# Gating unit's second half and all heads' values by seven block products, with a new order of retention

## What is computed

```python
h = _rmsnorm(x, g_pre_mix)
q, k, v, g, u, sv, gate_r, gate_s = split(h @ w_in)
# retention, 4 heads: q, k 128 wide, v, g 256 wide
o = _layernorm(retention(rotary(q), rotary(k), v))      # both directions, decay by distance
ret = (o * silu(g)) @ w_ret_o
# gating unit: u and sv are 1024 wide
u = gelu(u)
sv = _layernorm(gelu(sv), sgu_ln_g, sgu_ln_b)
sgu = (u * (w_spatial @ sv + b_spatial)) @ w_sgu_o      # mixes tokens within 128
x = x + rmsnorm(mixture of ret and sgu by sigmoid gates @ w_out)
x = x + rmsnorm(conv-gated mlp)
```

## Time and profile before

| what | value |
|---|---|
| median of the timed runs | 2129.3 us |
| time of the profiled execution | 2129.32 us |
| its span, first to last instruction | 2127.5 us |
| TensorE matmuls busy | 2117.5 us, 12356 |
| VectorE busy | 1698.5 us |
| ScalarE busy | 1098.1 us |
| share of TensorE in the chain that ended last | 96% |
| mean granted clock of TensorE | 0.999 |

### The profile page before, as it was taken

The page is one execution under the profiler, slowest core; times in us unless marked ns, Lnnn a source line. Parts: engine busy times, 40 slices in busy tenths (PEclk is TensorE's granted clock), DMA queues, the critical chain, the costliest instruction groups (busy, mean ns, idle before and its releaser), DMA issues.

```text
span 2127.5 us, 32016 instructions
## 1 busy us (share of the span) xinstructions
PE 2117.5 (100%) x12356; PEld 1854.2 (87%) x12356; DVE 1698.5 (80%) x2623; ACT 1098.1 (52%) x1824; POOL 135.4 (6%) x181
## 2 busy tenths in 40 slices
PE   9999999999999999999999999999999999999998
PEld 7888889999888888889999888888888899888887
DVE  7999988888867999988888866664766569877887
ACT  5788555555535788555555534332554344222354
POOL 0010001111010010001111010000000000000000
PEclk9999999999999999999999999999999999999999
DMA  5221246775333221237775333223232231222552
GB/s 196 71 82 63 91 122 177 179 194 152 110 114 112 74 79 63 97 117 178 180 189 155 110 114 129 99 79 118 91 107 70 99 139 46 99 93 98 188 178 99
DMA packets 61331, 252.64 MB, mean 119 GB/s; under 512 B 7520, under 2 KB 8288, under 8 KB 42784
## 3 DMA queue, kind: packets, MB, share of 16 engines
q1 hardware_dynamic: 47680, 223.72, 29.8%
q0 software_dynamic: 13248, 27.27, 7.8%
q10 hardware_dynamic: 288, 0.14, 0.0%
HBM read 245.19 MB, written 2.10 MB: 116 GB/s over the span
## 4 chain that ended last, share of the span: by engine, by line
PE 96%; DVE 2%; ACT 1%; DMA 0%; issue 0%; SPq 0%; DVEq 0%; ACTq 0%
PE mm L2780 20%; PE mm L2782 20%; PE mm L2781 20%; PE sp L2780 9%; PE sp L2782 9%; PE sp L2781 9%; PE ob L3065 1%; PE sp L3037 1%; PE sp L3052 1%; DVE conv_y L1757 1%; PE ob L3045 0%; PE sp L3054 0%; ACT probs L820 0%; PE misc L2780 0%; PE misc L2782 0%
## 5 line engine op out<-in xcount | busy, mean ns | idle before, releaser
L2780 PE MATMUL mm<-in_hi,w_hi 128*128 128x512 f32 (+1 forms) x1536 | 541.6, 353 | 0.4 <-DVE in_lo L1679 0.4
L2781 PE MATMUL mm<-in_lo,w_hi 128*128 128x512 f32 (+1 forms) x1536 | 536.7, 349 | 0.0
L2782 PE MATMUL mm<-in_hi,w_lo 128*128 128x512 f32 (+1 forms) x1536 | 536.7, 349 | 0.0
L2780 PEld LDWEIGHTS mm<-in_hi,w_hi 128*128 128x128 f32 x1536 | 288.9, 188 | 41.2 <-issue 3.4
L2782 PEld LDWEIGHTS mm<-in_hi,w_lo 128*128 128x128 f32 x1536 | 288.7, 188 | 37.8
L2781 PEld LDWEIGHTS mm<-in_lo,w_hi 128*128 128x128 f32 x1536 | 289.0, 188 | 36.1
L764 ACT ACTIVATE w_hi<-w_raw 128x2048 fp32r<-128x2048 f32 (+2 forms) x103 | 192.2, 1866 | 226.3 <-PE mm L2782 187.0
L1645 DVE TENSOR_TENSOR w_lo<-w_raw,w_hi 128x2048 fp32r<-128x2048 f32 (+1 forms) x102 | 224.6, 2201 | 87.2 <-ACT w_hi L764 78.9
L1013 ACT ACTIVATE w_hi<-w_raw 128x512 fp32r<-128x512 f32 x206 | 126.7, 626 | 188.7 <-DVE w_raw L2059 88.2
L2780 PE MATMUL sp<-in_hi,w_hi 128*128 128x256 f32 (+1 forms) x544 | 177.7, 327 | 0.0
L2782 PE MATMUL sp<-in_hi,w_lo 128*128 128x256 f32 (+1 forms) x544 | 177.4, 326 | 0.0
(11 more groups left out here) (574 smaller groups left out, 4849.0 us busy)
## 6 DMA issues: line engine op xcount, KB each, us to landing
w_raw<-in_w_dram SPq DMA_DIRECT2D x134, 1024.0 KB, 4.8
w_raw<-in_w_dram SPq DMA_DIRECT2D x85, 512.0 KB, 6.1
w_raw<-in_w_dram POOLq DMA_DIRECT2D x44, 256.0 KB, 4.2
w_third_sum<-in_w_dram SPq DMA_DIRECT2D x44, 256.0 KB, 6.4
w_third_sum<-in_w_dram POOLq DMA_DIRECT2D x44, 256.0 KB, 4.8
w_raw<-in_w_dram SPq DMA_DIRECT2D x8, 768.0 KB, 4.2
w_chain<-in_w_dram SPq DMA_DIRECT2D x6, 1024.0 KB, 6.5
w_chain<-in_w_dram POOLq DMA_DIRECT2D x4, 1024.0 KB, 9.4
```

Source lines behind the costliest of these rows:

```text
L2780: MM(out, ah, bh, start=first, stop=False, **kw)
L2781: MM(out, ah, bl, start=False, stop=False, **kw)
L2782: return MM(out, al, bh, start=False, stop=last, **kw)
```

## The change

- **sv and v** are each made by seven block products (Strassen's form) instead of eight: TOK_A11, A12, S1, S2, S4, S3, A22. A block has 256 tokens (two halves i of 128), four k-tiles and 512 columns. Some operands on the token side are x itself; four others (`token_operand_at`, o = 0 to 3) are sums and differences of x's quarters, made in `tks`, `tkh` and `tkl`: for each pair of k-tiles p one difference, one scaled copy, three sums, a high part each and a low part each. On the weight side S1 and S3 are sums made by accumulating loads (`tok_chain`), S2 and S4 are sums made by VectorE (`tok_first_sum`, `tok_second_sum`). The products are put together by ScalarE copies (`tok_copy`) and VectorE additions (`tok_take`), or by accumulating in the bank.
- **Order**: u's tiles 0 to 3 come first, with the square sum in the second one; then sv, then the values of all four heads (`token_matrix(1, TOK_V)`), then u's tiles 4 to 7. The last down product of the second layer gets the first instructions for the new operands in between.
- **The variance** of sv is taken between two weight parts of the values; the four normalisations are spread behind it. The centring of the values and the decay tables move beside the gating unit's output.
- **Retention** loses its value products. q and k of the next head stand ahead of the weighing of this head; score weights are made for two token blocks at once in a tensor of their own (`rpf`), and the outputs are copied out of the banks by ScalarE, not VectorE.
- **SP and POOL**: loads of the two matrices wait for semaphores of their own; POOL issues four accumulating loads of 1 MB. There are as many weight chunks as before.

The diff, cut to its core:

```diff
-S_SV, S_U, S_SGU, S_RET, S_AR, S_RO, S_OUT, S_UP, S_DOWN = 4, 4, 8, 12, 4, 4, 4, 22, 14
+S_SV, S_V, S_U, S_SGU, S_RET, S_AR, S_RO, S_OUT, S_UP, S_DOWN = 4, 4, 4, 8, 8, 4, 4, 4, 22, 14
...
+TOK_SV, TOK_V, TOK_END = 2, 9, 16
+TOK_A11, TOK_A12, TOK_S1, TOK_S2, TOK_S4, TOK_S3, TOK_A22 = range(7)
+DOWN_DONE = 7 * FT + D_SPOTS
+PLAIN_DONE = 7 * FT + D_SPOTS - N_SPOTS
...
+            e.wait_ge(s_sm, (DEPTH - 1) * DOWN_DONE + PLAIN_DONE)
+            sv_w, v_w, u_w = n + 2, n + 2 + S_SV, n + 2 + S_SV + S_V
...
+            for i in range(2):
+                tok_load(tok_chain[i], sv_w + 2, s_k[i])
...
-            for t, src in ((gtab, SGT[:, 0:D]), (btab, SGT[:, D:2 * D]), (bsp, sg[:, 0]), (wspr, sg[:, 1])):
+            for t, src in ((btab, SGT[:, D:2 * D]), (bsp, sg[:, 0]), (wspr, sg[:, 1])):
...
+            e.wait_ge(s_w, made(0))
+            tok_load(raw[:, 0, :], sv_w, s_raw[0])
+            e.wait_ge(s_w, made(1))
+            tok_load(raw[:, 1, :], sv_w + 1, s_raw[1])
+            e.wait_ge(s_mmf, DEPTH * L_MM + 2 + 1)
+            e.dma_start(gtab, SGT[:, 0:D]).then_inc(s_tab, 16)
+            e.wait_ge(s_bs, 1)
+            tok_load(raw[:, 0, :], sv_w + 3, s_raw[0])
+            e.wait_ge(s_w, made(TOK_SV + TOK_S1))
+            tok_load(tok_chain[0], v_w + 2, s_k[0])
+            e.wait_ge(s_bs, 2)
+            tok_load(raw[:, 1, :], v_w, s_raw[1])
+            e.wait_ge(s_w, made(TOK_SV + TOK_S3))
+            tok_load(tok_chain[1], v_w + 2, s_k[1])
+            e.wait_ge(s_w, made(TOK_SV + TOK_A22))
+            tok_load(raw[:, 0, :], v_w + 1, s_raw[0])
...
+            sv_w = DEPTH * L_CHUNKS + 2
+            for m, c in enumerate((sv_w, sv_w + S_SV)):
+                for i, part in ((0, 3), (1, 0)):
+                    e.wait_ge(s_k[i], 16 * (m + 1))
+                    e.dma_start(tok_chain[i], W[c + part:c + part + 1].rearrange("a p c -> (a p) c"),
+                                accum_op=ALU.add).then_inc(s_ka[i], 16)
...
+                def token_first_high(p):
+
+                    e.wait_ge(s_td, p + 1)
+                    e.activation(tkh[:, p, 0, :], tks[:, p, 1, :], ACT.Copy,
+                                 scale=minus_gn[:, 2 * p:2 * p + 1]).then_inc(s_t1, 1)
+                    e.activation(tks[:, p, 2, :], x[:, 2 * p + 1, second_half], ACT.Copy,
+                                 scale=parl[:, A_GN + 2 * p + 1:A_GN + 2 * p + 2]).then_inc(s_t1, 1)
+
+                def token_sums_high(p):
+
+                    e.wait_ge(s_tq, 3 * (p + 1))
+                    e.activation(tkh[:, p, 1:4, :], tks[:, p, 1:4, :], ACT.Copy).then_inc(s_t2, 1)
...
                                 next_high(m)
+                            if l == DEPTH - 1:
+                                for p in range(HK - 1):
+                                    token_first_high(p)
...
+                if l == DEPTH - 1:
+                    token_sums_high(0)
...
+            def tok_high_after(u, src):
+                e.wait_ge(s_bd, tok_part(u - 2, 1))
+                tok_high(u, src)
+
+            def tok_high_loaded(u):
+                e.wait_ge(s_raw[u % 2], raws[u % 2].next(16))
+                tok_high_after(u, raw[:, u % 2, :])
+
+            def tok_copy(u, i, src, dst):
+                e.wait_ge(s_bd, tok_part(u, i))
+                e.activation(dst, src, ACT.Copy).then_inc(s_bc, 1)
...
-            e.wait_ge(s_tab, 64)
+            token_sums_high(1)
+            e.wait_ge(s_msf, misc_taken.next())
+            inverse_root(tD[:], rstd[:], signal=root)
+            token_sums_high(2)
+            token_first_high(HK - 1)
+            tiles.skip(2)
+            prep(0)
+            token_sums_high(HK - 1)
+            e.wait_ge(s_mmf, taken.next(2))
+            for m in range(2):
...
+            u0 = TOK_SV
+            tok_copy(u0 + TOK_A11, 0, tok_x[0][0], tok_copy_1[0][0])
+            tok_copy(u0 + TOK_A11, 1, tok_x[0][1], tok_copy_1[0][1])
+            e.wait_ge(s_ka[0], 16)
+            tok_high_after(u0 + TOK_S1, tok_chain[0])
+            e.wait_ge(s_bs, 1)
+            tok_high_after(u0 + TOK_S2, tok_sum)
...
+            u0 = TOK_V
+            tok_high_loaded(u0 + TOK_A12)
             e.preload_act_table_set(LN_EXP)
+            for i in range(2):
+                tok_copy(u0 + TOK_A11, i, tok_x[1][i], tok_copy_1[1][i])
             e.wait_ge(s_val, val.next())
             inverse_root(mv[:, :, 1:2], mv[:, :, 1:2])
-            for c in range(S_U):
+            e.wait_ge(s_ka[0], 32)
+            tok_high_after(u0 + TOK_S1, tok_chain[0])
...
+                def token_difference(p):
+
+                    e.wait_ge(s_val, val.now())
+                    TT(tks[:, p, 1, :], x[:, 2 * p, second_half], x[:, 2 * p, first_half], ALU.subtract).then_inc(s_td, 1)
+
+                def token_sums_of(p):
+
+                    g, minus = col(parl, A_GN + 2 * p), minus_gn[:, 2 * p:2 * p + 1]
+                    t2, t3, t4 = (tks[:, p, o, :] for o in (1, 2, 3))
+                    e.wait_ge(s_t1, 2 * p + 2)
+                    STT(tkl[:, p, 0, :], t2, minus, r32(tkh[:, p, 0, :]), ALU.mult, ALU.subtract).then_inc(s_tt, 1)
+                    STT(t2, t2, g, t3, ALU.mult, ALU.subtract).then_inc(s_tq, 1)
+                    e.wait_ge(s_tq, 3 * p + 1)
+                    STT(t3, x[:, 2 * p, second_half], minus, t3, ALU.mult, ALU.add).then_inc(s_tq, 1)
+                    STT(t4, x[:, 2 * p + 1, first_half], minus_gn[:, 2 * p + 1:2 * p + 2], t2,
+                        ALU.mult, ALU.subtract).then_inc(s_tq, 1)
+
+                def token_sums_low(p):
+
+                    e.wait_ge(s_t2, p + 1)
+                    TT(tkl[:, p, 1:4, :], tks[:, p, 1:4, :], r32(tkh[:, p, 1:4, :]), ALU.subtract).then_inc(s_tt, 1)
...
+                        if j == 2 and l == DEPTH - 1:
+                            e.wait_ge(s_sm, (DEPTH - 1) * DOWN_DONE + PLAIN_DONE)
+                            for q in range(HK - 1):
+                                token_difference(q)
                         if j == 3:
                             for m in (2, 3, 4, 5):
                                 in_lo(m, col(parl, m + A_GN))
+                        if j == 4 and l == DEPTH - 1:
+                            token_sums_of(0)
...
+            def tok_first_sum(slot, m):
+                e.wait_ge(s_ka[0], 16 * (m + 1))
+                e.wait_ge(s_w, w_out.now())
+                TT(tok_sum, tok_chain[0], raw[:, slot, :], ALU.add).then_inc(s_bs, 1)
+
+            def tok_second_sum(slot):
+                TT(tok_sum, tok_sum, raw[:, slot, :], ALU.add).then_inc(s_bs, 1)
+
+            def tok_take(u, i, dst, bank, other, copied):
+                e.wait_ge(s_bd, tok_part(u, i))
+                e.wait_ge(s_bc, copied)
+                TT(dst, bank, other, ALU.add).then_inc(s_bt, 1)
...
+            token_sums_of(1)
             mean_square(D, tD[:])
             e.memset(ssum[:], 0.0).then_inc(s_do, own.up())
...
+            token_sums_low(0)
+            token_sums_of(2)
+            token_sums_low(1)
+            token_difference(HK - 1)
+            token_sums_low(2)
+            e.wait_ge(s_rs, 1)
+            take(us[:, 0, :], 0)
+            take(us[:, 1, :], 1)
+            token_sums_of(HK - 1)
+            prep(0)
+            token_sums_low(HK - 1)
+            take(us[:, 2, :], 0)
+            take(us[:, 3, :], 1)
+            prep(1)
+            e.wait_ge(s_o, o_in.next())
+            TS(rt[:], ob[:, 0:T:P], 1.0, None, ALU.mult).then_inc(s_of, o_taken.up())
+            e.wait_ge(s_of, o_taken.now())
+            TS(minus_rt, rt[:], -1.0, None, ALU.mult).then_inc(s_of, o_taken.up())
+            e.wait_ge(s_of, o_taken.now())
+            e.wait_ge(s_mmf, taken.now())
+            tok_first_sum(0, 0)
+            u0 = TOK_SV
+            tok_low(u0 + TOK_S1, tok_chain[0])
+            tok_low(u0 + TOK_S2, tok_sum)
+            tok_second_sum(1)
             for i in range(2):
-                prep(0)
...
+                piece(2 + i, 0)
+            u0 = TOK_V
+            tok_low_raw(u0 + TOK_A12)
+            tok_first_sum(1, 1)
+            for i in range(2):
+                piece(2 + i, 1)
+            for i in range(2):
+                piece(i, 1)
...
             TS(mv[:, :, 1:2], mv[:, :, 1:2], EPS, None, ALU.add).then_inc(s_val, val.up())
+            tok_low(u0 + TOK_S1, tok_chain[0])
+            e.wait_ge(s_w, w_out.now())
+            for i in range(2):
+                tok_take(u0 + TOK_A12, i, v_pair(0, i), two_heads(tok_y[1][i]), two_heads(tok_copy_1[1][i]), 7 + i)
+            tok_low(u0 + TOK_S2, tok_sum)
+            tok_second_sum(0)
+            tok_low(u0 + TOK_S4, tok_sum)
             e.wait_ge(s_tab, 64)
...
+                prep(0)
+                e.wait_ge(s_sub, sub.now())
+                take(og[:, 2 * hd, :], 0)
+                if hd:
+                    output_variance()
+                take(og[:, 2 * hd + 1, :], 1)
+                if hd:
+                    gate_output(hd - 1)
```

(151 more changed lines are left out.)

496 lines of the change are left out of this document (298 added, 198 removed).

## The result

The changed kernel takes 2166.3 us in the median (six runs, 2165.2 to 2170.6) against 2129.35: 1.0176 times the time before, 95% interval 1.0166 to 1.0185. Forecast were 2135.0 us and a range up to 2140.5. So it is slower, as was said, but by 36.9 us and not by 5.7. The profiled execution took 2165.54 us, its span is 2163.8.

What follows compares the result with a forecast made beforehand. TensorE, busy 2117.5 of 2127.5 us, was taken as the bound. 2129.3 - 12.8 (matmuls) + 10.7 (join) + 4.7 (block waits) + 3.1 (clock) = 2135.0 us, range 2126.5 to 2140.5.

Steps and rivals of the forecast that it cites:

- TensorE's work: Matmul time removed by seven blocks per matrix: gating half 5.4 us, values 7.4 us, together -12.8 us.
- The join: Between the layers and this block, VectorE's added work makes TensorE wait in u's first tiles: 10.7 us, bounds 4 and 12.
- the tB sum: At the join, the first u tile waits for this VectorE sum: 3.7 us.
- the take of us 0: At the join, the third u tile reuses bank mm0 and waits for VectorE to empty it: 5.4 us.
- The waits on in_lo and sum_lo: At the join, first u tile waits for its last low input, 0.5 us; second for the sum of squares, 1.0 us.
- S1 of the values: In the values' blocks, statistics and inverse root ahead of S1's parts make TensorE wait 4.5 us.
- S4 of the gating half: S2's low part and the second weight sum delay ScalarE's start on S4's weights: 0.2 us late.
- The clock: TensorE's clock falls after the waits of 5.4 and 4.5 us: up to 3 us each, 3.1 us taken for both.
- The six us of work at half speed: Upper end of the clock estimate, 3 us per wait; the middle was taken.
- Retention: Heads take 29.9 us of TensorE instead of 41.3, with no new waits: 0, upper bound 2 us.
- SP, POOL and the loads: Chunk loads and accumulating loads of the two matrices arrive in time: 0 to 2 us, 0 taken.
- The rival of late loads: Chunk for the values' A12 loads late beside an accumulating load, lengthening the wait at S1: 2137 to 2140 us, chance 0.12.

Runs made afterwards that it cites:

- e6_join: e5_both with the rest of the join's waits taken out (u's first tiles, banks, first gating weights, low parts and takes reordered); 2117.3 us.
- e3_var: e1_count with the gating unit's variance moved: last statistics behind the low part of S1 of the values, inverse root behind S4's high part; 2130.8 us.
- e5_both: e1_count with both the variance moved as in e3_var and the token operands' work moved behind the join's root and takes; 2121.9 us.
- e1_count: The changed kernel with SP's counter of finished weight parts advanced by 13 instead of 14 behind the last load of the values; 2136.4 us.

## Why the prediction was wrong, point by point

- **TensorE's work: right.** The values' 384 small products gone from retention give 45.4 us, by the stages; seven blocks, with no wait but 0.15 us ahead of S4, take 38.4 in e6_join (1344.10 to 1382.49). The gating half takes 38.5 for 43.5. Forecast were 7.4 and 5.4; 7.0 and 5.0 came, and e6_join, where nearly nothing waits, comes within 0.8 us of 2129.3 - 12.8.
- **The join: right.** The forecast had waits of 3.7 on the tB sum (3.6 came), 5.4 on the take of us 0 (5.0) and the third u tile from 1304.8 (1303.74). In all 10.7 and the clock's 1.6 were counted, 12.1 came. The waits on in_lo and sum_lo, 1.5 us, did not come: TensorE ran at half clock just ahead of them (next section), which cost about as much and had it arrive later.
- **S1 of the values: right.** 4.5 forecast, 4.2 came; e3_var shows that the root and the statistics ahead of S1 are its cause. The 0.2 us ahead of S4 of the gating half came as 0.15, and the first product behind it took 0.1 more.
- **The clock: right in the main.** 3.1 us were counted for two falls; these cost 1.4 and 2.2, seven and eleven slow products. A third, behind the wait on the tB sum, cost 1.4; the prediction allowed for it and gave it no price, because what follows waits for VectorE anyway, and so it came. The six us of work at half speed, from which the middle was taken, stood in no row; seven and eleven products are 3.0 and 4.7 us.
- **Retention: right.** Heads follow each other in 30.43 us without a wait. The forecast of 29.9 forgot the 0.5 us of the sum's products, which the heads before had too (1506.30 to 1548.09 is 41.79, not 41.3).
- **SP, POOL and the loads: the step that failed.** It said "nothing is late: 0 to 2 us, I take 0", and looked at the loads of the two matrices alone, each against its own deadline. Of the plain chunk loads behind them it says nothing, so they count as before in its sum. But they wait by a running count, and a change that takes some loads out of the count must move it by exactly the right number; whether it does can be worked out from the diff. It was not. The rival of late loads (2137 to 2140) had the right engine, a deadline of single loads as its mechanism, and 2 to 5 us where the count costs 29.9. Without the count the changed kernel measures 2136.4, 1.4 from the forecast. That it comes so near is in part luck: a wait of 0.8 us on msgu, ahead of the gating unit's output, was not forecast, and the last block began 0.9 us earlier than in the kernel before, which was not forecast either.

Had the count been seen, its price could have been estimated from the kernel before: in the output stage and in the row phase a chunk lasts 5.4 to 5.7 us, while load, high and low part in a row make 4.7 + 1.9 + 2.3, 9. That is some 3.5 us for each of the four or so chunks in a stage that find nothing finished ahead, in two stages.

## What to carry to other kernels

A wait on a running count ties each later instruction of a queue to everything that was skipped before it. So where a change moves loads out of a counted sequence, the count behind them is worked out anew, slot by slot, and then held against the stage with the shortest chunk, however far behind the change it lies: a delay that hides under 10.9 us a chunk shows under 5.5. In a trace, a load that is issued only when the engine that needs it is already idle is its mark. And work that nobody needs soon goes behind the takes and roots that free TensorE, never ahead of them: two such moves in VectorE's and ScalarE's queues brought 14.5 us here (e5_both against e1_count).

## What the runs showed of the hardware

Products at half clock, of which the kernel before has no row, cost 0.427 us for 512 columns, against 0.2267. TensorE's timeline of the changed kernel at the third u tile (start, duration):

```profile
1303.74 0.77 PE L3083 MATMUL mm<-in_hi,w_hi 128*128 128x512 f32 x1 [4.96 <-DVE u_gelu L1848]
1304.30 0.63 PE L3084 MATMUL mm<-in_lo,w_hi 128*128 128x512 f32 x1
1304.73 0.63 PE L3085 MATMUL mm<-in_hi,w_lo 128*128 128x512 f32 x1
...
1307.36 0.39 PE L3083 MATMUL mm<-in_hi,w_hi 128*128 128x512 f32 x1
```

And the clock of its surroundings, with that of the first gap of the join (1281.63 to 1285.52) ahead:

```profile
1285.00:1286.00 1.00, 0.48 (x2) 0.47 (x3) 1.00 (x2) 0.00 (x0) 0.00 (x0) 1.00 0.00 0
1286.00:1287.00 1.00, 1.00 (x5) 0.72 (x4) 0.97 (x3) 0.00 (x0) 0.00 (x0) 0.72 0.00 0
1287.00:1288.00 1.00, 1.00 (x4) 0.80 (x3) 1.00 (x3) 0.00 (x0) 0.00 (x0) 0.50 0.00 0
...
1303.00:1304.00 1.00, 0.26 (x1) 0.29 (x2) 1.00 (x2) 0.07 (x1) 0.00 (x0) 0.75 0.96 262
1304.00:1305.00 1.00, 1.00 (x3) 0.81 (x3) 0.98 (x3) 0.00 (x0) 0.00 (x0) 0.50 0.97 262
1307.00:1308.00 1.00, 1.00 (x6) 0.83 (x5) 0.00 (x0) 1.00 (x1) 0.00 (x0) 1.00 1.04 434
```

Two things were not expected. After the first gap the clock fell from 2.4 to 1.2 GHz only when TensorE was at work again, about 1 us into the tile: a gap's price falls on the matmuls behind it, which appear in no list of waits. Gaps here run from the start of the last product to the start of the next. In the second gap the clock had fallen just ahead of the restart at 1303.74: the row from 1303 to 1304 has 0.75. And the price doesn't depend on the gap's length in a way that these rows show: 3.9 and 5.35 us of gap cost seven slow products each (7 x 0.20 = 1.4 us), 4.56 us eleven (2.2). Nor is it the same for a gap of that length in the same place in another run: in e3_var the second one, 5.42 us from 1298.69 to 1304.11, has its clock down earlier and thirteen slow products behind it.

```profile
1302.00:1303.00 1.00, 0.00 (x0) 0.00 (x0) 1.00 (x3) 0.64 (x3) 0.00 (x0) 0.91 0.97 270
1303.00:1304.00 1.00, 0.00 (x0) 0.00 (x0) 1.00 (x3) 0.44 (x2) 0.00 (x0) 0.50 1.07 295
```

In the row phase a shorter gap did it too: behind one of 2.20 us (2057.72 to 2059.92) eight slow products begin at 2061.21, with the clock at 0.63 from 2061 to 2062; behind the next one, 2.09 us (2066.91 to 2069.00), there are none. In the output stage, after a gap of 4.41 us in the changed kernel, twenty products of 256 columns follow each other at 0.213 us instead of 0.118, and sixteen more after one of 3.5. Together with the 8.5 us for which TensorE stood still there these 3.4 us make up the 12.7 by which the stage grew, but for 0.8. The Trainium skill (TensorE: Matmul & The Clock Gate, section Why this matters for your kernels) says that gaps between bursts cost the clock and that steady work brings it up again; the trace agrees for all the gaps above but that of 2.09 us, and here the way back shows as well: 0.50 from 1304 to 1305, 1.00 again from 1307 to 1308.
